# Eight conditioning groups move from the sample attention to the first MLP and the short convolution

## The chip, the cores and the metric

The kernel runs on one core of a Trainium2 chip. The core has a matrix engine (TensorE), a vector engine (VectorE), an activation engine (ScalarE), GpSimd (POOL in the profile) and a sync engine (SP) that issues transfers. All of them run their own instruction streams and meet at semaphores. The metric is the device time of one execution in microseconds.

## The reference

The program is one inference step of a two-layer decoder trunk in fp32. A prompt of 256 tokens and 8 samples of 8 new tokens each (320 tokens in all) pass through the same weights. Model width is 2048, MLP width 8192. Four times (mixer and MLP of layer 0, mixer and MLP of layer 1) the input is normalised and modulated by a vector that depends on the condition `c`:

```python
def ada_modulate(c, w, b):
    m = jax.nn.silu(c) @ w + b                       # (2048) @ (2048 x 6144)
    shift, scale, gate = jnp.split(m[:, None, :], 3, axis=-1)
def modulated_norm(x, g, shift, scale):
    return rmsnorm(x, g) * (1.0 + scale) + shift
for layer in range(2):
    shift, scale, gate = ada_modulate(c, ada_mix_w[layer], ada_mix_b[layer])
    h = modulated_norm(x, norm_mix[layer], shift, scale)
    y = even_mixer(h, ...) if layer == 0 else odd_mixer(h, ...)
    x = x + gate * y
    shift, scale, gate = ada_modulate(c, ada_mlp_w[layer], ada_mlp_b[layer])
    x = x + gate * sq_relu_mlp(modulated_norm(x, norm_mlp[layer], shift, scale), w1, w2)
```

The even mixer is differential attention beside a gated recurrence; for the samples, the attention reads 256 past positions for each sample from a paged cache. The odd mixer is a short convolution: `b, c, x = split(h @ w_in, 3)`, then `(b * conv3(c * x)) @ w_out`. There are nine conditions (one of the prompt, eight of the samples), so each of the four modulations is a product of 9 rows with a 2048 x 6144 matrix: much weight, little arithmetic.

## The kernel before

**Weights of the layers.** Every large product is done with 128x128 stationary tiles in a split form: a weight chunk (128 partitions x 4 x 256 values, 512 KB) lands in one of four `raw` slots (`load`, L346), ScalarE rounds it to `w_hi` (`split`, L537), VectorE writes the rest to `w_lo` (`split`, L885), and TensorE does three products for each tile: hi by hi, hi by lo, lo by hi (`pair`, L1505). A pair is four chunks, 96 matmuls of 320 columns, and gives 256 output columns. Chunks flow on in one order for the whole kernel, counted by the tallies `K`; the sync engine issues them in program order.

**The modulations.** Each of the four is 12 groups of 512 output columns, 48 in all. A group is 16 tiles of 128x512 weights. `ada_tile_in` (L1539) puts tile k in strip k mod 4 of the bank `acc`, with 32 columns of the condition as the stationary part. After 16 tiles ScalarE copies `acc` to `ares` (`ada_out`, L551), TensorE sums the four strips by four small matmuls into `folded` (`fold`, L1565), and VectorE adds the bias and writes `mod` (`ada_bias`, L932). The tiles come by one of two rings. The wide ring has eight slots of two tiles (512 KB each); in this part it lies in the memory of `w_hi` and `w_lo`, so it serves only while no layer weights are split. The narrow ring has four slots of one tile (256 KB) beside the layer weights; its tiles are executed in bursts of four between chunks (`turn_with_ada`, L376, L1095, L1575), one group for 8 chunks.

Where the groups are computed: 8 of the first modulation at the start, 4 more and 4 of the second in the first projection, 8 of the second in the attention (head norms and prompt), 8 of the third in the sample stage, 4 of the third in block 0 of the first MLP and the 12 of the fourth in its blocks 1 to 3. The short convolution and the second MLP compute none.

**The sample stage** (L1765 to L1810 of TensorE, L772 to L779 of ScalarE, L1361 to L1388 of VectorE, L492 to L510 of POOL). For each sample TensorE computes scores against the transposed past keys, VectorE scales and finds the maximum, ScalarE takes the exponential, VectorE normalises, TensorE combines and transposes the two softmaxes, VectorE copies the weights to `s_pt`, and TensorE multiplies them with the value pages. The 16 key transposes of the next sample (`s_keys`) stand between. The next sample's scores wait for the evacuation of this one's weights. POOL issues the pages: value pages of sample b when the values of b - 2 are done, then the key pages of b + 1. Between these steps stand four pieces of a group (`ada(wide_later, ...)`) of four tiles each, and the fold of the group before. The wide slabs are issued by the sync engine when a slot is free; then come the first chunks of the output projection.

**The short convolution** (TensorE L1875 to L1882, ScalarE L843 to L850, VectorE L1449 to L1486): 8 turns of three pairs, 12 chunks each. VectorE forms the product of the first two pairs, runs the three taps, and multiplies with the third pair. Pair 2 uses the bank that also holds `folded`.

Of the kernel before, what the change touches and what calls it, by code (L numbers as in the profile page):

```python
# [13 lines left out]
P = 128  # L14
D = 2048
KT = D // P
# [104 lines left out]
@contextmanager  # L121
def looped(eng, lo, hi, per):

    if hi - lo == 1:
        yield lo
        return
    before = [(t, t.base, t.off) for t in per]
    with eng.Fori(lo, hi) as i:
        for t, base, off in before:
            t.base, t.off = base + i * per[t], off - lo * per[t]  # L130
        yield i
    for t, base, off in before:
        added = t.off - (off - lo * per[t])
        assert added == per[t], f"a turn adds {added}, not {per[t]}"
        t.base, t.off = base, off + (hi - lo) * per[t]

def trunk_kernel(nc, A, O):
    with ExitStack() as ctx:
# [108 lines left out]
        aux = ctx.enter_context(nc.psum_tensor("aux", [P, 2, 512], F32))  # L248
        acc = aux[:, 1, :]
        folded = mm[:, 2, 1, 448:448 + 4 * NC]  # L250

        def C(name, rows=P):
            return const[0:rows, COL[name][0]:COL[name][1]]
# [81 lines left out]
        ADA = [A["ada_mix_w"][0], A["ada_mlp_w"][0], A["ada_mix_w"][1], A["ada_mlp_w"][1]]  # L335
        ADA_B = [ROW["ada_mix_b"], ROW["ada_mlp_b"], ROW["ada_mix_b"] + 48, ROW["ada_mlp_b"] + 48]
        GAIN = [ROW["norm_mix"], ROW["norm_mlp"], ROW["norm_mix"] + KT, ROW["norm_mlp"] + KT]
        MOD_READY = [8, 24, 48, 48]
        H_READY = [0, 8, 12, 16]
        X_READY = [1, 9, 41, 49, 81]  # L340

# [1 line left out]
        def _(sp):  # L343
# [10 lines left out]
            def load_quad(src):  # L354
                for s in range(SLOTS):
                    load(src(s))
# [60 lines left out]
            sp.wait_ge(chunk_used, 80)  # L417
            with looped(sp, 4, GROUPS, {KW: 8}) as g:
                ada_wide(wide_later, 1, g)
            with looped(sp, 0, 8, {KW: 8}) as g:  # L420
                ada_wide(wide_later, 2, g)
            for half in halves:
                for s in (0, 1):
                    load(half(s))
# [25 lines left out]
                    load_quad(slab(W1, 0, after))  # L450

            load_quad(slab(A["mlp_w1"][0], 0, 0))
            feed_with_ada(0, 2, 8, D)
            with looped(sp, 1, BLOCKS - 1, {K: 64, KN: 64}) as b:
                feed_with_ada(b, 3, b * 4 - 4, (b + 1) * D)
            feed_with_ada(3, 3, 8, None)
            with looped(sp, 1, KT // 2 + 1, {K: 12}) as j:
                end = sp.snap(j * COLS)
                for part in (1, 2, 0):
                    load_quad(slab(A["w_in_odd"][0], 0, end + (part * D - COLS)))  # L460
            matrix(A["w_out_odd"][0], 8)
            with looped(sp, 0, BLOCKS, {K: 64}) as b:
                feed_forward(1, b)

# [67 lines left out]
        def _(act):  # L532
# [240 lines left out]
            for b in range(NB):  # L773

                act.wait_ge(s_max, b + 1)
                fn(s_s[:, :], s_s[:, :], ACT.Exp, bias=small[:, 0, 8:9], accum_out=small[:, 0, 9:10]).then_inc(s_exp, 1)
                if b + 1 < NB:
                    s_keys(b + 1)
                ada_out(True)  # L779
            act.wait_ge(s_o, NB)  # L780
            for n in range(4):
                ins = fn(s_kT[:, n // 2, P * (n % 2):P * (n % 2) + P], aux[:, 0, P * n:P * n + P], ACT.Square,
# [26 lines left out]
            squared(0)  # L809
            mixed(3)  # L810
            squared(1)
            act.wait_ge(wide_used, 8 * 24)
            split(1)
            rooted(0)
            split(1)
# [24 lines left out]
            root()  # L840
            norm()
            G.off = 20 + 8 + 32
            with looped(act, 0, KT // 2, {K: 12, G: 3}) as j:  # L843
                split()
                multiplied()
                fn(mtmp[:, 0], mm[:, 0, :, 0:T], ACT.Copy).then_inc(c_copied, 1)
                split(8)
                G.up(3)
                act.wait_ge(pair_free, G.now + 2)
                fn(u_hi[:, bass.ds(j * 2, 2), :], mtmp[:, 1], ACT.Copy).then_inc(u_hi_ready, 1)  # L850
# [20 lines left out]
        def _(dve):  # L871
# [57 lines left out]
            AG, X, R, SQ = Tally(), Tally(), Tally(), Tally()  # L929
            X.off = 1  # L930

            def ada_bias(a, g):  # L932
# [4 lines left out]
                v.tensor_tensor(mod[:, a, bass.ds(g * 4, 4), :], folded.rearrange("p (t c) -> p t c", c=NC), bias,  # L937
                                ALU.add).then_inc(mod_ready, 1)

# [170 lines left out]
            def mlp(n, last, groups=0):  # L1111
                def hidden(r, j):

                    R.up()
                    dve.wait_ge(relu_out, R.now)
                    v.tensor_tensor(mtmp[:, r], mtmp[:, r], mtmp[:, r], ALU.mult).then_inc(u_val, 1)  # L1116
                    U.up()
                    dve.wait_ge(u_hi_ready, U.now)
                    v.tensor_tensor(u_lo[:, bass.ds(j, 2), :], mtmp[:, r], u_hi[:, bass.ds(j, 2), :].bitcast(F32),  # L1119
                                    ALU.subtract).then_inc(u_ready, 1)  # L1120

                def block_(ahead, group=None, squares=False):
                    if group is not None:
                        a, g0 = group
                        with looped(dve, 0, 4, {K: 8, R: 2, U: 2, AG: 1}) as i:
                            turn_with_ada(lambda: hidden(0, i * 4), lambda: hidden(1, i * 4 + 2), a, g0 + i)
                    else:
                        with looped(dve, 0, 4, {K: 8, R: 2, U: 2}) as i:
                            split()
                            hidden(0, i * 4)  # L1130
                            split()
                            hidden(1, i * 4 + 2)
                    if ahead:
                        outward(n, squares)
                    else:
                        with looped(dve, 0, 3, {K: 8, G: 2, X: 2, steps: 2}) as i:
                            split()
                            residual(0, i * 4, n)
                            split()
                            residual(1, i * 4 + 2, n)  # L1140
                        split()
                        residual(0, 12, n)
                        residual(1, 14, n, ahead=0)

                per = {G: 8, R: 8, U: 8, X: 8, steps: 8}
                if groups:
                    block_(1, (2, 8))
                    with looped(dve, 1, BLOCKS - 1, {K: 64, AG: 4, **per}) as b:
                        block_(1, (3, b * 4 - 4))
                    block_(1, (3, 8), squares=True)  # L1150
# [211 lines left out]
            for b in range(NB):  # L1362
# [10 lines left out]
                step(v.tensor_tensor(small[:, 0, 11:12], small[:, 0, 10:11], lam[:, 1:2], ALU.mult))  # L1373
                settle()
                v.tensor_scalar(s_s[:, :], s_s[:, :], small[:, 0, 11:12], None, ALU.mult).then_inc(s_w, 1)
                if b:
                    ada_bias(2, b - 1)
                if b + 1 < NB:
                    s_keys(b + 1)
                dve.wait_ge(s_wT, b + 1)  # L1380
# [1 line left out]
                if b:  # L1382
# [2 lines left out]
                v.tensor_copy(s_pt[:, 0:2, :, now:now + 8], mm[:, 2, 0, 0:P].rearrange("p (a h q) -> p a h q", a=2, h=H))  # L1385
                v.tensor_copy(s_pt[0:TS, 2, :, now:now + 8], mm[0:TS, 2, 0, P:P + 64].rearrange("p (h q) -> p h q", h=H)
                              ).then_inc(s_pte, 1)
            ada_bias(2, NB - 1)  # L1388

            dve.wait_ge(s_root, 1)  # L1390
            step(v.reciprocal(small[:, 1, 12:16], small[:, 1, 12:16]))
# [54 lines left out]
            step(v.memset(c_p[:, :, 0:2], 0.0))  # L1446
            norm()
            Z = Tally()
            with looped(dve, 0, KT // 2, {K: 12, G: 3, U: 1, steps: 5, Z: 1}) as j:  # L1449
                split(8)  # L1450
                multiplied()
                Z.up()
# [23 lines left out]
                            ins = v.scalar_tensor_tensor(out_s, c_s[:, m, :, k:k + DS], w, out_s, ALU.mult, ALU.add)  # L1476
                    step(ins)
                settle()
                split()
                multiplied()  # L1480
                G.up()
                v.tensor_tensor(mtmp[:, 1], mtmp[:, 1], mm[:, 2, :, 0:T], ALU.mult).then_inc(pair_free, 1)
# [15 lines left out]
        def _(pe):  # L1498
# [63 lines left out]
                    ada_tile_in(k, narrow[:, slot, :]).then_inc(narrow_used, 1)  # L1562
                    KN.up()

            def fold():  # L1565

                if not (isinstance(F.now, int) and F.now == 0):
                    pe.wait_ge(mod_ready, F.now)
                F.up()
                pe.wait_ge(ada_copied, F.now)  # L1570
                for t in range(4):
                    ins = mul(folded[:, NC * t:NC * t + NC], ares[:, P * t:P * t + P], C("fold"), True, True)
# [194 lines left out]
            for b in range(NB):  # L1767
# [12 lines left out]
                        h = 2 * j + a  # L1780
                        ins = mul(mm[32 * j:32 * j + 32, 2, 0, PAST:T], s_q[:, h, :], pj[:, 8 + h, SEQ:T], a == 0, a == 1)
                ins.then_inc(s_score, 1)
                if b:
                    fold()
                ada(wide_later, range(2))
                if b + 1 < NB:
                    s_keys(b + 1)
                ada(wide_later, range(2, 4))
                pe.wait_ge(s_w, b + 1)
                for k in range(3):  # L1790

                    rows, at_col = P if k < 2 else TS, 64 * k
                    ins = mul(mm[0:rows, 2, 0, at_col:at_col + 64], s_s[:, P * k:P * k + rows], C("comb"), True, True)
                ins.then_inc(s_wT, 1)
                ada(wide_later, range(4, 6))
                pe.wait_ge(s_pte, b + 1)
                pe.wait_ge(values_in[b % 2], 32 * (b // 2 + 1))
                for half in range(2):
# [7 lines left out]
                                                   keys[:, P * h:P * h + P], start=b == half == k == 0,  # L1806
                                                   stop=b == NB - 1 and k == 2, skip_group_check=True)
                ins.then_inc(s_o, 1)
                ada(wide_later, range(6, 8))
            fold()  # L1810
            pe.wait_ge(mod_ready, F.now)
            pe.wait_ge(s_norm, 1)
            for n in range(4):
# [59 lines left out]
            norm()  # L1873

            def three(inputs=None):  # L1875
                for r in range(3):
                    pair(r, h_hi, h_lo, inputs if r == 0 else None, (pair_free, G.now))

            three(h_inputs(12))
            with looped(pe, 1, KT // 2, {K: 12, G: 3}):  # L1880
                three()
            pair(0, u_hi, u_lo, lambda s: pe.wait_ge(u_ready, 32 + 2 * s + 2))  # L1882

            for j in range(KT):
                bank = aux[0:18, j // 4, :] if j < 8 else mm[0:18, 2, (j - 8) // 4, :]
                ins = turn(bank[:, P * (j % 4):P * (j % 4) + P], stage[:, j, :])
# [51 lines left out]
```

## Time and profile before

| | us |
|---|---|
| median of the runs shown (3301.89 to 3309.1) | 3304.24 |
| the profiled execution, its own time | 3302.08 |
| its span, first to last instruction | 3300.4 |

| engine | busy, us | share |
|---|---|---|
| TensorE matmuls | 3127.5 | 95% |
| VectorE | 1520.6 | 46% |
| ScalarE | 1087.9 | 33% |
| POOL | 29.6 | 1% |

The span is that of one profiled execution. Positions below (as 617 us) count from its start. Busy time of TensorE is modelled for pipelined matmuls. A matmul of plain fp32 operands shows as two instructions, so four conditioning tiles are a row with x8. [...]

### The profile page before, as it was taken

What the parts mean: (1) busy time and instruction counts of PE and PEld (TensorE: products, weight loads), DVE (VectorE), ACT (ScalarE), POOL (GpSimd) and SP (SyncE); (2) the same over time, 40 slices, a digit from 0 to 9 for tenths busy, and PEclk for the clock granted to TensorE, in tenths of its full rate; (3) what the DMA queues carried; (4) which work ended last, traced back from release to release, by engine and by line L of the source; (5) the groups of instructions that cost most, each with busy time, mean ns of one, the idle gap of its engine ahead of it and who ended that gap; (6) DMA issues with size and microseconds to landing.
All of it is one profiled execution on the core that took longest, in us unless ns stands there. A gap on an engine that the chain in (4) does not pass through costs nothing.

```text
span 3300.4 us, 55870 instructions
## 1 busy us (share of the span) xinstructions
PE 3127.5 (95%) x21283; PEld 2857.2 (87%) x21283; DVE 1520.6 (46%) x2047; ACT 1087.9 (33%) x1302; POOL 29.6 (1%) x55
## 2 busy tenths in 40 slices
PE   6899996888899999999999899999899999999998
PEld 2588873448789989989989899999899999999998
DVE  1535656336634434434434554445644444444443
ACT  1324423223433233233233243333433333333332
POOL 0000000000000000000000000000000000000000
PEclk9899997889899999999999999999899999999999
DMA  9777768884475575575575444444344444444443
GB/s 349 245 253 231 231 234 297 305 323 130 146 253 181 177 245 183 177 247 185 173 251 187 133 128 148 151 147 148 114 152 148 147 147 153 147 147 152 143 152 108
DMA packets 512228, 624.34 MB, mean 189 GB/s; under 512 B 22416, under 2 KB 408081, under 8 KB 511444
## 3 DMA queue, kind: packets, MB, share of 16 engines
q1 hardware_dynamic: 504576, 595.68, 55.7%
q0 software_dynamic: 6112, 22.84, 1.9%
q10 hardware_dynamic: 1430, 4.24, 0.4%
q8 instruction: 83, 1.36, 0.2%
q14 instruction: 27, 0.22, 0.0%
HBM read 617.13 MB, written 5.54 MB: 189 GB/s over the span
## 4 chain that ended last, share of the span: by engine, by line
PE 89%; DVE 4%; DMA 4%; ACT 1%; issue 1%; SPq 0%; DVEq 0%; POOL 0%; ACTq 0%; POOLq 0%
PE mm L1503 83%; PE aux L1503 5%; DMA wide_first<-in_ada_mix_w 2%; DMA wide_later<-in_ada_mix_w 2%; DVE a_rr L1279 1%; PE mm L1611 1%; SPq L364 0%; DVE l_g L1407 0%; PE aux L1805 0%; ACT tmp L631 0%; DVE a_qn L1282 0%; DVE pj L1290 0%; DVE p_s L1306 0%; DVE a_t L1288 0%; DVE rstd L944 0%
## 5 line engine op out<-in xcount | busy, mean ns | idle before, releaser
L890 DVE TENSOR_TENSOR w_lo<-raw,w_hi 128x1024 fp32r<-128x1024 f32 x752 | 919.3, 1225 | 1406.2 <-ACT w_hi L544 1404.7
L544 ACT ACTIVATE w_hi<-raw 128x1024 fp32r<-128x1024 f32 x752 | 795.3, 1059 | 1690.3 <-PE mm L1503 1690.3
L1503 PE MATMUL mm<-h_hi,w_hi 128*128 128x320 f32 x3712 | 1166.1, 314 | 47.6 <-DVE h_lo L986 32.3
L1503 PE MATMUL mm<-h_lo,w_hi 128*128 128x320 f32 x3712 | 1152.0, 310 | 0.0
L1503 PE MATMUL mm<-h_hi,w_lo 128*128 128x320 f32 x3712 | 1151.8, 310 | 0.0
L1503 PEld LDWEIGHTS mm<-h_hi,w_hi 128*128 128x128 f32 x3712 | 701.9, 189 | 133.7 <-issue 123.0
L1503 PE MATMUL mm<-u_hi,w_hi 128*128 128x320 f32 x2304 | 712.0, 309 | 0.0
L1503 PE MATMUL mm<-u_lo,w_hi 128*128 128x320 f32 x2304 | 711.9, 309 | 0.0
L1503 PE MATMUL mm<-u_hi,w_lo 128*128 128x320 f32 x2304 | 711.9, 309 | 0.0
L1503 PEld LDWEIGHTS mm<-h_lo,w_hi 128*128 128x128 f32 x3712 | 702.2, 189 | 0.0
L1503 PEld LDWEIGHTS mm<-h_hi,w_lo 128*128 128x128 f32 x3712 | 701.6, 189 | 0.0
L1503 PEld LDWEIGHTS mm<-u_hi,w_hi 128*128 128x128 f32 x2304 | 432.4, 188 | 0.0
L1503 PEld LDWEIGHTS mm<-u_lo,w_hi 128*128 128x128 f32 x2304 | 432.4, 188 | 0.0
L1503 PEld LDWEIGHTS mm<-u_hi,w_lo 128*128 128x128 f32 x2304 | 432.4, 188 | 0.0
L1503 PE MATMUL aux<-wide_later,cs 128*32 128x512 f32 x512 | 95.2, 700 | 15.7 <-DMA wide_later<-in_ada_mix_w 13.7
L1503 PE MATMUL aux<-narrow,cs 128*32 128x512 f32 x768 | 106.6, 609 | 0.0
L1119 DVE TENSOR_TENSOR u_lo<-mtmp,u_hi 128x640 f32 x64 | 52.8, 826 | 67.0 <-ACT u_hi L660 67.0
L1503 PE MATMUL aux<-wide_first,cs 128*32 128x512 f32 x256 | 61.0, 825 | 22.1 <-DMA wide_first<-in_ada_mix_w 21.3
L660 ACT ACTIVATE u_hi<-mtmp 128x640 f32 x64 | 47.3, 739 | 98.6 <-DVE mtmp L1116 98.6
L559 ACT ACTIVATE ares<-aux 128x512 f32<-128x512 f32 x48 | 28.6, 595 | 134.0 <-PE aux L1503 133.8
L1072 DVE SCALAR_TENSOR_TENSOR xT<-mm,mod,xT 128x256 f32 (+1 forms) x160 | 69.4, 475 | 0.0
L1503 PEld LDWEIGHTS aux<-wide_first,cs 128*32 128x32 f32 x256 | 10.5, 133 | 64.9 <-DMA wide_first<-in_ada_mix_w 47.7
(262 smaller groups left out, 1236.5 us busy)
## 6 DMA issues: line engine op xcount, KB each, us to landing
raw<-in_mlp_w SPq DMA_DIRECT2D x512, 512.0 KB, 3.6
narrow<-in_ada_mlp_w SPq DMA_DIRECT2D x256, 256.0 KB, 3.6
raw<-in_w_in_odd SPq DMA_DIRECT2D x96, 512.0 KB, 3.9
raw<-in_w_in_even SPq DMA_DIRECT2D x80, 512.0 KB, 6.6
wide_first<-in_ada_mix_w SPq DMA_DIRECT2D x64, 512.0 KB, 8.8
narrow<-in_ada_mix_w SPq DMA_DIRECT2D x128, 256.0 KB, 4.0
wide_later<-in_ada_mlp_w SPq DMA_DIRECT2D x64, 512.0 KB, 5.1
wide_later<-in_ada_mix_w SPq DMA_DIRECT2D x64, 512.0 KB, 11.2
```

The lines of the kernel that those rows point to most:

```text
L544: fn(w_hi[:, slot], raw[:, slot], ACT.Copy).then_inc(hi_ready, 1)
L559: fn(ares[:, :], acc, ACT.Copy).then_inc(ada_copied, 1)
L660: fn(u_hi[:, bass.ds(j, 2), :], mtmp[:, r], ACT.Copy).then_inc(u_hi_ready, 1)
L890: v.tensor_tensor(w_lo[:, slot], raw[:, slot], w_hi[:, slot].bitcast(F32), ALU.subtract).then_inc(lo_ready, 1)
L1072: ins = v.scalar_tensor_tensor(x, mm[:, r, m, 0:SEQ], g, x, ALU.mult, ALU.add)
L1119: v.tensor_tensor(u_lo[:, bass.ds(j, 2), :], mtmp[:, r], u_hi[:, bass.ds(j, 2), :].bitcast(F32), ALU.subtract).then_inc(u_ready, 1)
L1279: step(v.reciprocal(a_rr[:, i % 2], a_rt[:, i % 2]))
L1503: return nc.tensor.matmul(out, lhsT, rhs, start=first, stop=last)
L1611: return nc.tensor.transpose(out, in_, const[0:rows, 0:rows])
```

## The change

The eight groups of the third modulation leave the sample stage. The first MLP computes the third modulation whole in blocks 0 to 2 and the first four groups of the fourth in block 3; the other eight groups of the fourth are computed in the eight turns of the short convolution, one group a turn, with four tiles before every third chunk and the fold after the eleventh. There the fold writes to another bank (`folded_conv`), since pair 2 uses the old one. The sync engine's order in the convolution becomes four narrow tiles and three chunks, four times a turn.

```diff
+        folded_conv = aux[:, 0, 448:448 + 4 * NC]
-        MOD_READY = [8, 24, 48, 48]
+        MOD_READY = [8, 24, 40, 48]
 # sync
-            with looped(sp, 0, 8, {KW: 8}) as g:
-                ada_wide(wide_later, 2, g)
-            feed_with_ada(0, 2, 8, D)
+            feed_with_ada(0, 2, 0, D)
             with looped(sp, 1, BLOCKS - 1, {K: 64, KN: 64}) as b:
-                feed_with_ada(b, 3, b * 4 - 4, (b + 1) * D)
-            feed_with_ada(3, 3, 8, None)
+                feed_with_ada(b, 2, b * 4, (b + 1) * D)
+            feed_with_ada(3, 3, 0, None)
+            def conv_turn(end, g, after):
+                sources = [slab(W_ODD, 0, end + (part * D - COLS))(s) for part in (2, 0) for s in range(SLOTS)]
+                sources += [after(s) for s in range(SLOTS)]
+                for n in range(4):
+                    ada_narrow(3, g, range(4 * n, 4 * n + 4))
+                    for src in sources[3 * n:3 * n + 3]:
+                        load(src)
...
 # scalar: sample stage, then convolution
-                ada_out(True)
-            act.wait_ge(wide_used, 8 * 24)
+            act.wait_ge(wide_used, 8 * 16)
-                split(8)
+                split(5)
+                ada_out()
+                split(3)
 # vector: sample stage, then convolution
-                if b:
-                    ada_bias(2, b - 1)
-            ada_bias(2, NB - 1)
-                split()
+                split(3)
+                ada_bias(3, j + 4, folded_conv)
+                split(1)
 # tensor: sample stage
-                if b:
-                    fold()
-                ada(wide_later, range(2))
-                ada(wide_later, range(2, 4))
-                ada(wide_later, range(4, 6))
-                ada(wide_later, range(6, 8))
-            fold()
 # tensor: convolution
             def three(inputs=None):
                 for r in range(3):
-                    pair(r, h_hi, h_lo, inputs if r == 0 else None, (pair_free, G.now))
+                    def burst(s):
+                        c = 4 * r + s
+                        if c % 3 == 0:
+                            ada_narrow(range(4 * (c // 3), 4 * (c // 3) + 4))
+                    pair(r, h_hi, h_lo, inputs if r == 0 else None, (pair_free, G.now), before=burst,
+                         between=(lambda s: fold(folded_conv) if s == 2 else None) if r == 2 else None)
...
+            pe.wait_ge(mod_ready, F.now)
             for j in range(KT):     # the 16 transposes of the convolution's new state
```

## Rows read from the trace of the kernel before

**Rows 1.** The page: busy time by engine; the chain of waits by engine.
```profile
PE 3127.5 (95%) x21283; PEld 2857.2 (87%) x21283; DVE 1520.6 (46%) x2047; ACT 1087.9 (33%) x1302; POOL 29.6 (1%) x55
PE 89%; DVE 4%; DMA 4%; ACT 1%; issue 1%; SPq 0%; DVEq 0%; POOL 0%; ACTq 0%; POOLq 0%
```

**Rows 2.** Stretches: length, busy us by engine (PE first), granted clock, DMA share, GB/s.
```profile
555.00:565.00 10.00, 6.98 (x32) 4.30 (x32) 3.77 (x11) 2.73 (x10) 0.00 (x0) 0.50 0.88 310
...
616.00:640.00 24.00, 20.13 (x272) 11.18 (x272) 9.02 (x33) 3.92 (x7) 5.17 (x10) 1.00 0.96 348
...
665.00:680.00 15.00, 11.94 (x128) 6.08 (x127) 2.45 (x11) 1.31 (x4) 2.11 (x4) 0.77 1.04 393
...
1900.95:2244.00 343.05, 343.05 (x2323) 343.05 (x2324) 174.15 (x256) 118.97 (x123) 0.00 (x0) 0.99 0.47 145
...
924.24:958.04 33.80, 33.80 (x234) 29.67 (x233) 13.03 (x13) 11.74 (x14) 0.00 (x0) 1.00 0.77 248
```

**Rows 3.** The chain of waits, 610 to 780 us, shares by line.
```profile
by line: DMA wide_later<-in_ada_mix_w 35.0%; PE mm L1503 19.5%; PE aux L1503 14.3%; DVE l_g L1407 6.0%; PE aux L1805 5.9%; PE mm L1611 5.5%; DVE w_lo L890 3.4%; issue 2.2%; DVE h_lo L1401 1.7%; DVE pj L1409 1.7%; SPq L364 0.9%; ACT h_hi L79
```

**Rows 4.** The chain, in order of time: start, length, what; both MLPs.
```profile
923.25 1.00 PE aux L1503 x8
924.24 7.23 PE mm L1503 x48
...
948.92 8.12 PE mm L1503 x56
...
2379.98 220.59 PE mm L1503 x1504
```

**Rows 5.** Instructions in time, sample 0: start, us, engine, line, operation [idle before].
```profile
617.18 1.07 PE L1503 MATMUL mm<-s_kT,s_q 128*32 128x256 f32 x16 [1.93 <-DVE s_q L1357]
...
618.53 0.42 DVE L1364 TENSOR_SCALAR s_s<-mm 128x256 f32<-128x256 f32 x1 [1.50 <-PE mm L1503]
...
619.76 0.56 ACT L776 ACTIVATE s_s<-s_s,small 128x320 f32<-128x320 f32 x1 [4.33 <-DVE small L1369]
...
620.45 0.16 DVE L1371 RECIPROCAL small<-small 128x1 f32<-128x1 f32 x1 [0.72 <-ACT s_s L776]
...
620.85 0.39 DVE L1375 TENSOR_SCALAR s_s<-s_s,small 128x320 f32<-128x320 f32 x1
...
622.40 0.53 DVE L1357 COPY s_q<-pj 64x32 f32<-64x32 f32 x4
...
623.31 0.21 DVE L1386 COPY s_pt<-mm 64x64 f32<-64x64 f32 x1
...
623.88 0.62 PE L1805 MATMUL aux<-vpage,s_pt 128*32 128x128 f32 x16
...
625.36 0.42 PE L1805 MATMUL aux<-vtok,s_pt 64*32 64x128 f32 x8
```

**Rows 6.** The same view behind the last sample.
```profile
730.80 0.27 ACT L782 ACTIVATE s_kT<-aux 128x128 f32<-128x128 f32 x1
```

**Rows 7.** The same view, sample 3, before and after a pause of TensorE.
```profile
660.34 1.06 PE L1503 MATMUL aux<-wide_later,cs 128*32 128x512 f32 x8
...
667.35 1.92 PE L1503 MATMUL aux<-wide_later,cs 128*32 128x512 f32 x4 [1.86 <-DMA wide_later<-in_ada_mix_w]
...
670.59 1.07 PE L1805 MATMUL aux<-vpage,s_pt 128*32 128x128 f32 x8
...
674.39 0.42 PE L1805 MATMUL aux<-vtok,s_pt 64*32 64x128 f32 x8
```

**Rows 8.** POOL's page issues; landing of the first key pages, then over the kernel.
```profile
626.11 0.53 POOL L508 DMA_DIRECT2D vpage<-in_cache_v  x1 [9.09 <-PE aux L1805]
626.99 0.53 POOL L508 DMA_DIRECT2D vpage<-in_cache_v  x1 [0.36 <-issue]
628.70 1.12 POOL L502 DMA_DIRECT2D kpage<-in_cache_k  x2 [1.18 <-issue]
...
DMA to landing us min/median/max: 3.9/4.2/4.6
...
kpage<-in_cache_k POOLq DMA_DIRECT2D x16, 512.0 KB, 9.0
```

More of the change, by code:

```diff
@@ L452, in _ @@
             load_quad(slab(A["mlp_w1"][0], 0, 0))
-            feed_with_ada(0, 2, 8, D)
+            feed_with_ada(0, 2, 0, D)
             with looped(sp, 1, BLOCKS - 1, {K: 64, KN: 64}) as b:
-                feed_with_ada(b, 3, b * 4 - 4, (b + 1) * D)
-            feed_with_ada(3, 3, 8, None)
-            with looped(sp, 1, KT // 2 + 1, {K: 12}) as j:
+                feed_with_ada(b, 2, b * 4, (b + 1) * D)
+            feed_with_ada(3, 3, 0, None)
+            W_ODD = A["w_in_odd"][0]
+            def conv_turn(end, g, after):
[5 more added lines that the diff above has]
+                        load(src)
+            load_quad(slab(W_ODD, 0, D))
+            with looped(sp, 1, KT // 2, {K: 12, KN: 16}) as j:
                 end = sp.snap(j * COLS)
-                for part in (1, 2, 0):
-                    load_quad(slab(A["w_in_odd"][0], 0, end + (part * D - COLS)))
-            matrix(A["w_out_odd"][0], 8)
+                conv_turn(end, j + 3, slab(W_ODD, 0, end + D))
+            conv_turn(KT // 2 * COLS, 11, slab(A["w_out_odd"][0], 0, 0))
+            matrix(A["w_out_odd"][0], 8, 1)
             with looped(sp, 0, BLOCKS, {K: 64}) as b:
@@ L842, in _ @@
             G.off = 20 + 8 + 32
-            with looped(act, 0, KT // 2, {K: 12, G: 3}) as j:
+            with looped(act, 0, KT // 2, {K: 12, G: 3, AG: 1, AN: 16}) as j:
                 split()
@@ L930, in _, with ada_bias @@
             X.off = 1
-            def ada_bias(a, g):
+            def ada_bias(a, g, out=folded):
                 AG.up()
@@ L936, in ada_bias @@
                 bias = vec[:, bass.ds(g * 4 + ADA_B[a], 4)].unsqueeze(2).broadcast_to([P, 4, NC])
-                v.tensor_tensor(mod[:, a, bass.ds(g * 4, 4), :], folded.rearrange("p (t c) -> p t c", c=NC), bias,
+                v.tensor_tensor(mod[:, a, bass.ds(g * 4, 4), :], out.rearrange("p (t c) -> p t c", c=NC), bias,
                                 ALU.add).then_inc(mod_ready, 1)
@@ L1146, in mlp @@
                 if groups:
-                    block_(1, (2, 8))
+                    block_(1, (2, 0))
                     with looped(dve, 1, BLOCKS - 1, {K: 64, AG: 4, **per}) as b:
-                        block_(1, (3, b * 4 - 4))
-                    block_(1, (3, 8), squares=True)
+                        block_(1, (2, b * 4))
+                    block_(1, (3, 0), squares=True)
                 else:
@@ L1448, in _ @@
             Z = Tally()
-            with looped(dve, 0, KT // 2, {K: 12, G: 3, U: 1, steps: 5, Z: 1}) as j:
+            with looped(dve, 0, KT // 2, {K: 12, G: 3, U: 1, steps: 5, Z: 1, AG: 1}) as j:
                 split(8)
@@ L1563, in ada_narrow, with fold @@
                     KN.up()
-            def fold():
+            def fold(out=folded):
                 if not (isinstance(F.now, int) and F.now == 0):
@@ L1571, in fold @@
                 for t in range(4):
-                    ins = mul(folded[:, NC * t:NC * t + NC], ares[:, P * t:P * t + P], C("fold"), True, True)
+                    ins = mul(out[:, NC * t:NC * t + NC], ares[:, P * t:P * t + P], C("fold"), True, True)
                 ins.then_inc(fold_done, 1)
@@ L1876, in three @@
                 for r in range(3):
-                    pair(r, h_hi, h_lo, inputs if r == 0 else None, (pair_free, G.now))
+                    def burst(s):
[4 more added lines that the diff above has]
+                         between=(lambda s: fold(folded_conv) if s == 2 else None) if r == 2 else None)
             three(h_inputs(12))
-            with looped(pe, 1, KT // 2, {K: 12, G: 3}):
+            with looped(pe, 1, KT // 2, {K: 12, G: 3, F: 1, KN: 16}):
                 three()
             pair(0, u_hi, u_lo, lambda s: pe.wait_ge(u_ready, 32 + 2 * s + 2))
+            pe.wait_ge(mod_ready, F.now)
             for j in range(KT):
```

## The prediction

> **What bounds the kernel now.** I read the page first: its engine totals and the chain of waits. TensorE is busy in 95% of the span and carries 89% of the chain [rows 1], so nearly everywhere a microsecond is won or lost only by changing what TensorE executes. Next I read stretches of the two places that the change touches [rows 2]. The short convolution (from 1900.95 us) is TensorE alone, 343.05 of 343.05 us busy at a granted clock of 0.99, while the transfers take 0.47 of their engines: whatever TensorE gets there is paid in full. The sample stage (617 to 731 us) is the other kind: its transfers stand at 0.96 to 1.04 of the engines, at 348 to 393 GB/s, and TensorE loses 3 to 4 us in each of two stretches of 24 and 15 us. The chain cut to 610 to 780 us says what it waits for: 35.0% of these 170 us, 59.5 us, is the landing of the wide slabs of the conditioning weights [rows 3]. Nothing in this stage reads what those slabs give; it needs only its own cache pages.
>
> So a bandwidth-bound stage gives up work which a TensorE-bound stage takes on. The answer is the difference of two numbers of nearly one size, and each has to be worked out.
>
> **What the convolution pays.** Each of its 8 turns gets 16 narrow tiles in four bursts of 4, a fold of 4 small matmuls, one copy on ScalarE, one bias add on VectorE and 16 DMAs of 256 KB. The first MLP already does just that in turns of 8 chunks, so it has the price. A turn with a group lasts 33.80 us [rows 2]. Plain turns go at 220.59 us for 1504 matmuls, 0.1467 us each [rows 4]; a turn has 8 chunks x 24 = 192, or 28.16 us. The group costs 33.80 - 28.16 = 5.64 us, and eight cost 45.1 us. The lower bound is the pieces of the chain alone: the burst's 1.00 us four times and 8.12 - 7.23 = 0.89 us for the fold [rows 4], 4.9 us a group or 39 us; the upper bound is 6 us a group, 48 us, should a burst or a fold have to wait a little in each turn. I take 5.64, since that row is the very same work.
>
> What hides the rest: ScalarE (118.97 of 343.05 us) and VectorE (174.15) are half idle in the convolution [rows 2], and copy and add sit between splits that are done before TensorE reaches their chunks, with two chunks (7 us) between the last burst and the fold against 0.6 us of copy. On the sync engine's queue a narrow tile waits for the burst before it, and the chunk loads queue behind it; the burst is every third chunk (10.8 us), where the MLP has every second (7.2 us), and there no turn is stretched. Bytes: 12 x 512 KB + 16 x 256 KB in 48 us is 220 GB/s, under the 248 GB/s of the MLP's turn. I cost these at nothing; uncovered, a late chunk would be a few us a turn. The MLP itself keeps 16 groups and is unchanged but for which groups they are. The new wait for the last bias add before the stage transposes has a whole pair (14 us) ahead of it: nothing.
>
> **What the sample stage gives back.** Out go 64 transfers of 512 KB (33.6 MB), 128 tiles, 8 folds, copies and adds. What stays is a serial chain for each sample. Sample 0 ran with pages and slabs already landed [rows 5]: scores from 617.18 us; VectorE from 618.53; ScalarE's exponential from 619.76; VectorE again from 620.45 to 621.24; its key copy and query copies to 622.93; the weights' copies to 623.52; values until 625.36 + 0.42 = 625.78. That is 8.60 us. Without a burst ahead of the combination, the 0.2 us before the weights' copies go, and a later sample adds a 0.22 us memset overlapped to 0.13, so 8.55 us; the next scores follow at once, since their wait is on those copies. Eight give 68.4 us: with every operation at full clock the last values end at 617.18 + 68.4 = 685.6 us. Before, the squares behind the last sample began at 730.80 us [rows 6], after a last burst and copy that also leave. Full gain 45.2 us. This is the convolution's price to within its error: at full clock the change is worth nothing.
>
> Two things can lengthen the 8.55 us. The first is the clock. Stretches with less TensorE work show it: 0.77 in 665 to 680 us, 0.50 in 555 to 565 us [rows 2]. [...] The new sample has TensorE active about 6.2 of 8.55 us: scores 1.3, transposes 1.95, then idle 0.9, combination 0.9, idle 1.4, values 2.1. Bursts filled both pauses before. At half clock, the scores add 1.0 us to the chain, the transposes end 1.15 us past the point where VectorE wants them, and values add 2.1: 4.2 us a sample, 34 us in all. The bounds are therefore 0 and 34 us; I take three tenths, 10.2 us, which is a granted clock of 0.85, between the 1.00 and 0.77 of the nearest rows, as the pauses are shorter than the 1.86 us that preceded the fall. [...]
>
> The second is the pages. Once a sample's values are done, POOL issues two value pages and, 2.6 us later, two key pages (626.11 and 628.70 us) [rows 8]. The key pages are wanted by the transposes of the second next sample's start, about 9.9 us after POOL's release, and at the latest 0.9 us later. Two pages alone landed in 3.9 to 4.6 us; with the slabs around them the median over the kernel is 9.0 us. At the lighter load, the last page is there some 8 us after the release: 2 MB in 8.55 us is 245 GB/s, against 393 reached. About 2 us are to spare, and I cost it at nothing; if landing stayed at 9 us from 629.8, each sample would wait 2 us, 12 us over six samples.
> [...]
>
> **Sum.** Against the profiled execution (span 3300.4 us, own time 3302.08): +45.1 in the convolution, -45.2 at full clock, +10.2 for the clock: +10.1 us, 3312.2 us. The median of the runs shown, 3304.24, lies 2.2 us above that execution; I put the forecast midway, 3313 us. Start and end of the kernel, attention over the prompt and both MLPs stay as they are.
>
> **Rivals.**
> The clock stays full (same): the sample takes 8.55 us; net 45.1 - 45.2 = 0, up to +4 with a spell or two: 3302 to 3306 us. For it: clock 1.00 from 616 to 640 us, with bursts [rows 2]. Against: those bursts go.
> The clock is low for most of the stage: 60% and more, 20 to 34 us, net +20 to +34: 3322 to 3336 us. For it: the 0.50 stretch of the prompt's attention, with longer pauses than here.
> The pages end last: +12 for pages beside some clock loss: about 3316 to 3328 us. Against it: 3.9 to 4.6 us landing when alone.
> Faster: the group costs the convolution only its pieces, 4.9 us, because the bursts' edges overlap the neighbouring matmuls better with three chunks between them. With full clock, that is 39.1 - 45.2 = -6.1 us; a sample chain of 8.3 us gives 2 more, -8: 3294 us. It decides from a group price under about 4.8 us. Against: 33.80 us for the MLP's turn, repeated in turn after turn.
>
> **How the numbers follow.** A measurement of this kernel tells from no change what exceeds 0.2%, 6.6 us. Forecast (part of the stage at half clock, +5 to +16) 0.50; clock full 0.20; clock mostly low 0.10; pages 0.08; faster 0.12. Slower by over 0.2%: 0.38 of the 0.50, all of low clock and 0.07 of pages, 0.55. Faster 0.12, the rest 0.33. The range leaves out the far end of the low clock and most of the faster case: 3298 to 3328 us; the forecast's own is 3307 to 3319.
>
> **What the profile after would show.** Convolution turns of 12 chunks at 42.2 + 5.6 = 47.9 us with TensorE always busy; a stage with no wait for wide slabs and transfers near 245 GB/s; the time from the first scores to the squares 68 us (clock full), about 79 us (forecast) or 100 us (clock low); TensorE's idle ended by VectorE's copies (right) or by page transfers (pages rival). I am wrong if the convolution's turns are under 47 us, if the stage stands at clock 1.00 and 68 us, or if a third place moves by over 3 us.

## The result, and the profile after

| us | before | after |
|---|---|---|
| median of the runs compared | 3303.06 (3298.26 to 3309.1, 4 runs) | 3321.18 (3320.14 to 3323.59, 4 runs) |
| the profiled execution's own time | 3302.08 | 3321.03 |
| its span | 3300.4 | 3319.4 |

The kernel after is slower: ratio 1.0055, 95% interval 1.0037 to 1.0073. The forecast was 3313 us with a range of 3298 to 3328, so sign and range hold, but the step is 18 to 19 us and not 10. Position by position, the two spans compare like this:

| stretch | before, us | after, us | difference |
|---|---|---|---|
| start to the first scores of the samples | 617.18 | 618.67 | +1.5 |
| first scores to the squares (sample stage) | 113.62 | 70.76 | -42.9 |
| squares to the first MLP's first matmul | 157.67 | 158.31 | +0.6 |
| first MLP and the norm behind it | 1012.48 | 1018.06 | +5.6 |
| short convolution, its output, the norm behind it | 472.33 | 515.77 | +43.4 |
| second MLP to the end | 927.12 | 937.83 | +10.7 |
| sum | 3300.4 | 3319.4 | +19.0 |

The two stretches that the change touches cancel to +0.6 us. The two MLPs, which execute the same number of matmuls as before, hold 16.3 of the 19.0 us.

The page after, in the order of [rows 1] (busy time by engine, the chain by engine), with the instruction queue of its third part between them (packets, MB, share):

```profile
PE 3135.1 (94%) x21283; PEld 2859.5 (86%) x21283; DVE 1521.0 (46%) x2047; ACT 1087.9 (33%) x1302; POOL 29.8 (1%) x55
...
q8 instruction: 108, 1.77, 0.2%
...
PE 90%; DVE 5%; DMA 2%; issue 1%; ACT 1%; SPq 0%; DVEq 0%; POOL 0%; ACTq 0%; POOLq 0%
```

The counts of TensorE's matmuls are those of [rows 1], as they should be in a pure move. The landing of the slabs has halved its share of the chain, and yet the whole is longer. One row of the kernel before, which [rows 1] had no use for, belongs beside this: its instruction queue moved 83 packets, and this one 108.

```profile
q8 instruction: 83, 1.36, 0.2%
```

Stretches after, with the columns of [rows 2]: the sample stage, the second turn of the convolution, a full-clock sample and the slow one behind it. The granted clock is TensorE's, as a share of its full speed.

```profile
618.67:689.43 70.76, 53.56 (x800) 36.90 (x800) 29.50 (x106) 11.60 (x24) 11.66 (x22) 0.85 0.51 180
1914.63:1962.51 47.88, 47.88 (x333) 43.75 (x336) 21.06 (x32) 14.64 (x15) 0.00 (x0) 1.00 0.70 220
...
626.73:634.87 8.14, 5.96 (x107) 4.30 (x110) 3.89 (x14) 1.56 (x3) 2.19 (x4) 1.00 0.70 260
634.87:644.26 9.39, 7.21 (x106) 4.77 (x110) 3.89 (x14) 1.56 (x3) 2.10 (x4) 0.84 0.68 226
```

The transfers of the stage fell from 0.96 to 1.04 of the engines [rows 2] to 0.51. The turn is 47.88 us, all of it TensorE.

Inside those two samples, TensorE in time (columns as [rows 5]):

```profile
634.80 1.07 PE L1514 MATMUL mm<-s_kT,s_q 128*32 128x256 f32 x16
...
638.92 0.92 PE L1514 MATMUL mm<-const,s_s 128*128 128x64 f32 x6 [0.93 <-DVE s_s L1387]
641.08 1.00 PE L1811 MATMUL aux<-vpage,s_pt 128*32 128x128 f32 x16 [1.24 <-DVE s_pt L1396]
...
644.19 1.93 PE L1514 MATMUL mm<-s_kT,s_q 128*32 128x256 f32 x16
...
651.54 0.65 PE L1811 MATMUL aux<-vpage,s_pt 128*32 128x128 f32 x16 [1.25 <-DVE s_pt L1396]
...
653.40 1.07 PE L1514 MATMUL mm<-s_kT,s_q 128*32 128x256 f32 x16
```

Both pauses, 0.93 and 1.24 us, end with VectorE's operations (the scaled weights `s_s`, then the copies to `s_pt`); no page ends one, so the pages rival is out. The same 16 value matmuls take 0.65 us at the higher level and 1.00 where the clock falls on the way, and the scores 1.07 or 1.93, as in the pair of [rows 7].

Now the part that I had called unchanged. The chain through the second MLP after (start, length, what):

```profile
2381.57 227.26 PE mm L1514 x1536
2608.83 1.25 issue
2610.08 1.56 PE mm L1514 x9
2611.63 2.27 issue
2613.90 225.76 PE mm L1514 x1527
2839.66 1.58 issue
2841.24 1.55 PE mm L1514 x9
2842.79 2.07 issue
2844.86 225.75 PE mm L1514 x1527
```

And the same piece of the kernel before, where the plain row of [rows 4] comes from:

```profile
2373.28 227.29 PE mm L1503 x1536
2600.57 1.73 issue
2602.29 225.52 PE mm L1503 x1536
2827.81 1.39 issue
2829.20 225.54 PE mm L1503 x1536
```

An MLP is a hardware loop over 4 blocks of 1536 matmuls for TensorE. At each jump back TensorE stops with nothing that it waits for ("issue"). Before, that is one stop of 1.4 to 1.7 us; after, there are two, nine matmuls apart. By the waits view TensorE's "issue" stops from 2300 us to the end add up to:

```profile
PE mm L1514 <- issue: 10.5, 6, 2.3
```

Before, it was 4.6 us in 3. So 5.9 of the 10.7 us are stops. The other 4.8 us is the speed behind them: behind the second stop the matmuls start 0.26 us apart and not 0.15, and the granted clock from 2613.90 to 2616.50 us is 0.54, half speed for nearly all of it,

```profile
2611.18 0.31 PE L1514 MATMUL mm<-h_lo,w_hi 128*128 128x320 f32 x1
2611.32 0.31 PE L1514 MATMUL mm<-h_hi,w_lo 128*128 128x320 f32 x1
2613.90 0.46 PE L1514 MATMUL mm<-h_hi,w_hi 128*128 128x320 f32 x1 [2.27 <-issue]
2614.16 0.47 PE L1514 MATMUL mm<-h_lo,w_hi 128*128 128x320 f32 x1
```

and 9 + 1527 matmuls take 1.56 + 225.76 = 227.32 us, where 1536 took 225.52 before (at the later two jumps the excess is 1.8 and 1.3 us). The first MLP had no stop at its jumps before. After, it has three, each just behind the 824 matmuls that end a block:

```profile
1097.73 2.00 issue
...
1348.15 1.65 issue
...
1598.11 1.31 issue
```

The change adds no TensorE instruction to either loop. What differs is the amount of TensorE code ahead of them, and with it the place where each loop lies in the instruction stream. The instruction queue moves more where there are more stops: 108 packets against 83 (16.4 KB each: 1.36 MB in 83). From these two I took the stops for fetches of instructions; no row names what a stop waits for.

### The profile page after: what moved, and what is told of

Read it like the earlier page. It is cut to its first block, busy times and chain, and to the rows that moved or that the text cites. A ratio compares the mean times of both kernels' runs of the same rounds, so it can differ in the third digit from the quotient of the medians.

```text
span 3319.4 us, 56069 instructions
## 1 busy us (share of the span) xinstructions
PE 3135.1 (94%) x21283; PEld 2859.5 (86%) x21283; DVE 1521.0 (46%) x2047; ACT 1087.9 (33%) x1302; POOL 29.8 (1%) x55
## 4 chain that ended last, share of the span: by engine, by line
PE 90%; DVE 5%; DMA 2%; issue 1%; ACT 1%; SPq 0%; DVEq 0%; POOL 0%; ACTq 0%; POOLq 0%
PE mm L1514 83%; PE aux L1514 6%; DMA wide_first<-in_ada_mix_w 2%; DVE a_rr L1291 1%; PE mm L1622 1%; PE aux L1811 1%; SPq L365 0%; ACT tmp L642 0%; DVE a_qn L1294 0%; DVE pj L1302 0%; DVE s_kT L1364 0%; DVE p_s L1318 0%; DVE l_g L1416 0%; DVE a_t L1300 0%; DVE rstd L956 0%
## 5 line engine op out<-in xcount | busy, mean ns | idle before, releaser
L1514 PE MATMUL aux<-narrow,cs 128*32 128x512 f32 x1024 | 141.6, 610 | 5.0 <-issue 5.0
L1514 PEld LDWEIGHTS aux<-wide_first,cs 128*32 128x32 f32 x256 | 10.2, 134 | 63.6 <-DMA wide_first<-in_ada_mix_w 45.2
L1514 PEld LDWEIGHTS mm<-const,ares 128*128 128x128 f32 x320 | 42.9, 203 | 14.3 <-issue 13.5
L1128 DVE TENSOR_TENSOR mtmp<-mtmp 128x640 f32<-128x640 f32 x64 | 52.4, 819 | 0.0
```

Of the source, the lines that this page charges most:

```text
L1514: return nc.tensor.matmul(out, lhsT, rhs, start=first, stop=last)
```

## Experiments

```diff
+MLP_LOOP = {False: dict(head_slot={mybir.EngineType.PE: 0}), True: dict(head_slot={mybir.EngineType.PE: 0})}
...
-                with looped(pe, 0, BLOCKS, {K: 64, G: 8, R: 8, UB: 8, F: groups, KN: 16 * groups}):
+                with looped(pe, 0, BLOCKS, {K: 64, G: 8, R: 8, UB: 8, F: groups, KN: 16 * groups}, MLP_LOOP[bool(groups)]):
```

> [...] Theory (layout): 16 of the 18 us that the change costs sit in the two MLPs, whose work is the same, as stalls of TensorE's instruction fetch where the block loop jumps back (2.00, 1.65, 1.31 us in the first MLP; 1.25+2.27, 1.58+2.07, 1.83+1.47 us in the second, where the second stall comes after 9 matmuls). With the head at the start of a fetch block the second stall goes: second MLP 937.8 -> 927 us or less, time 3306 to 3311 us. Rival (the moved transfers or the fuller sync queue disturb the MLPs): the same 3321 us, the stalls stay.

Measured: 3298.54 us (3294.85 to 3300.52), ratio to before 0.9982 (0.9973 to 0.9992); the kernel after without this line stood at 1.0055. The chain through the second MLP is one piece:

```profile
2375.31 903.40 PE mm L1517 x6144
```

The page counts 55 instruction packets. The expectation had only the second stop going; all of them went, in the first MLP too (1012.35 us, as in the kernel before), and the time is 7 us below the expected range.

```diff
+MLP_LOOP = {False: dict(hint_back_edge=True), True: dict(hint_back_edge=True)}
```

> [...] Theory (layout): all stalls at the turn of a block go, 5 us in the first MLP and 10 to 12 in the second: 3303 to 3308 us. [...] Rival (transfers): 3321 us.

Measured: 3299.96 us (3294.29 to 3301.47), ratio 0.9983 (0.9973 to 0.9992), and again one piece, of 903.51 us, with 54 instruction packets. Two different options, the same effect, 3 us below the expected range.

**The kernel before, spoiled.** If the place of the loops is the cause, the kernel before must fall to it too, with no group moved.

```diff
+MLP_LOOP = {False: dict(head_slot={mybir.EngineType.PE: 235}), True: dict(head_slot={mybir.EngineType.PE: 235})}
```

> [...] Theory (layout): the kernel before gets the changed kernel's stalls, a double stall in the second MLP (+9 to +11 us) and one or two in the first (+5 to +11 us): 3315 to 3325 us with the sample stage and the convolution untouched. Rival (transfers): 3303 us.

Measured: 3330.33 us (3327.78 to 3331.9), ratio 1.0077 (1.0061 to 1.0094), 111 instruction packets. The chain shows the double stop, in the second MLP

```profile
2390.18 226.80 PE mm L1506 x1536
2616.98 2.08 issue
2619.06 1.56 PE mm L1506 x9
2620.61 1.79 issue
2622.41 226.98 PE mm L1506 x1527
2849.38 1.87 issue
```

and in the first, at each of its three jumps; this is the first of them, with one burst of the narrow ring between the two stops:

```profile
1137.28 2.10 issue
1139.38 1.07 PE aux L1506 x8
1140.44 1.89 issue
```

This is the test that the rival can't pass: 25 us from the place of the code alone. With the heads at slot 235 a second stop stands nine matmuls into the body of the second MLP's loop; the kernel before had none there. The time is 5 us above the expected range: by the profiles the second MLP grew by 11.9 us and the first by 18.8, where I had allowed it 5 to 11.

**The kernel before with the jump announced, and aligned.**

```diff
+MLP_LOOP = {False: dict(hint_back_edge=True), True: dict(hint_back_edge=True)}
```

> The kernel before with the branch hint on both block loops. Theory (layout): the three stalls of the second MLP (1.73, 1.39, 1.45 us) go and the first MLP, which has none, stays: 3298 to 3300 us. If a hint costs more than it saves: 3303 us or more.

Measured: 3297.02 us (3290.97 to 3300.44), ratio 0.9973 (0.9963 to 0.9983), 1 us below the expected range.

And with the line of the first experiment, slot 0, in the kernel before:

> The kernel before, with both block loops of TensorE at the start of a fetch block, as e1 has them; no work is moved. It is the partner of e1_after_slot0: the difference of the two is the move alone. Stage sums from the profiles so far (sample stage 113.6 -> 72.5 us, convolution with its output 472.3 -> 516.3, both MLPs equal) give e1 minus e5 = +1 to +5 us; so e5 at 3294 to 3298 us. Rival (with the stalls gone, the move gains): e5 above e1.

Measured: 3295.76 us (3292.82 to 3300.0), ratio 0.998 (0.997 to 0.9989). So the kernel before also paid for its loops, some 7 us. With that taken out on both sides, the price of the move is what is left between equal options: by medians 3298.54 - 3295.76 = +2.8 us aligned (by spans 3297.1 - 3293.8 = +3.3) and 3299.96 - 3297.02 = +2.9 us announced. The announced pair is from one set; the aligned pair is not, and each against the kernel before of its own set leaves +0.8 us. All of it is within 0.2%, no change that can be told.

**The stage without its groups, and nothing in their place.** The aligned kernel before, minus the eight groups of the third modulation; they are computed nowhere, and their columns of `mod` are zero.

```diff
-            with looped(sp, 0, 8, {KW: 8}) as g:
-                ada_wide(wide_later, 2, g)
...
-                if b:
-                    fold()
-                ada(wide_later, range(2))
...
-                ada(wide_later, range(2, 4))
...
-                ada(wide_later, range(4, 6))
...
-                ada(wide_later, range(6, 8))
-            fold()
```

> As e5, but the eight groups of the sample stage are left out and computed nowhere (their columns of the third modulation are zeros): the removal alone. Theory: the stage from the first scores to the squares falls from 113.6 to 68 to 74 us (8.14 us a sample at full clock, 65 us, and some spells at half clock), nothing else moves: 40 to 45 us under e5, 3250 to 3257 us. Rival: part of the gain is given back later, in the output projection or by the first MLP's loads: under 38 us.

Measured: 3254.72 us (3250.03 to 3257.44), ratio 0.9852 (0.9836 to 0.9869). This splits the +2.8 us in its two terms: leaving the stage gives 3295.76 - 3254.72 = 41.0 us, entering the convolution costs 3298.54 - 3254.72 = 43.8 us (medians of two sets; by the profiles the stretch of the convolution grew from 472.58 to 516.27 us, 43.7). The stage itself fell from 113.40 to 73.67 us. The stage's clock is low here as well, so the low clock comes with the emptier stage and not with anything in the convolution:

```profile
615.25:688.92 73.67, 55.95 (x800) 37.26 (x800) 29.49 (x106) 11.60 (x23) 11.58 (x22) 0.82 0.48 172
```

**The pauses filled.** The aligned kernel after, with four small matmuls of constants into the unused `acc` in each of the two pauses of a sample (8 in the rows, two for each, as the 24 groups of 16 tiles from the narrow ring are 768 rows in the kernel before). They add work to TensorE and nothing else.

```diff
+            def filler():
+                for k in range(4):
+                    ada_strip = slice(32 * k, 32 * k + 32)
+                    mul(acc[ada_strip, :], cs[:, k, :], const[:, 0:GCOLS], True, True)
```

> As e1, with two bursts of four meaningless matmuls (cs by const into the idle bank acc, 1.0 us each) for each sample, one ahead of the combination and one ahead of the values, where TensorE pauses; no transfers. Theory (clock): TensorE's pauses let its clock fall in some samples; filled, the clock stays at 1.00 and the stage lasts 65 to 67 us instead of 72.5: 5 to 7 us under e1. Rival (the long samples of the stage are late pages): no change, or longer by the bursts.

Measured: 3291.5 us (3287.03 to 3296.39), ratio 0.9966 (0.9956 to 0.9976), 7.0 us under the same kernel without them by medians of two sets, and some 5 us when each is held against the kernel before of its own set. The stretch of its stage:

```profile
615.55:680.16 64.61, 60.99 (x928) 35.28 (x928) 29.49 (x106) 11.61 (x24) 11.72 (x22) 1.00 0.56 197
```

TensorE is busy 61.0 us and not 53.6, the clock is 1.00 throughout, and the stage is 6.2 us shorter than the 70.76 us of the kernel after (and 7.9 than the 72.48 us of the aligned one). The clock's price is shown by itself, and best by the stage. It also shows what the move is worth at full clock: 3291.5 - 3295.76 = -4.3 us against the aligned kernel before (one set; 0.13%, at the edge of what the intervals can tell).

**Work that counts in the pauses.** If small matmuls in the pauses keep the clock, useful ones may do so too: two of the eight groups, four tiles a sample in the second pause, can stay there as the filler, with a quarter of the slabs' bytes. The convolution then has six turns with a group and two without.

```diff
             # sync
+            with looped(sp, 0, 2, {KW: 8}) as g:
+                ada_wide(wide_later, 2, g)
             # tensor, sample stage
+                if b == 4:
+                    fold()
...
                 pe.wait_ge(s_w, b + 1)
...
+                ada(wide_later, range(2 * (b % 4), 2 * (b % 4) + 2))
                 pe.wait_ge(s_pte, b + 1)
...
             # tensor, convolution
-            with looped(pe, 1, KT // 2, {K: 12, G: 3, F: 1, KN: 16}):
+            with looped(pe, 1, 6, {K: 12, G: 3, F: 1, KN: 16}):
                 three()
+            with looped(pe, 6, 8, {K: 12, G: 3}):
+                three(with_group=False)
```

> As e1, but two groups of the third modulation stay in the sample stage (one burst of four tiles a sample, in the pause ahead of the values, from wide slabs) and six groups of the fourth run in the convolution's first six turns. Pages and slabs are 25.2 MB, 64 us at 393 GB/s, so the stage should hold 66 to 76 us and the convolution gives back 2 x 5.6 = 11.3 us: 8 to 14 us under e1, 3285 to 3291 us, under both given kernels. Rival: the slabs delay the pages and the stage grows by 11 us or more: no gain on e1.

Measured: 3283.86 us (3283.66 to 3285.34), ratio 0.9941 (0.9924 to 0.9958): 0.6% under the kernel before. Part of that is the aligned loops; against the aligned kernel before, from the same set, it is 3295.76 - 3283.86 = 11.9 us, 0.4%. The time is 1 us below the expected range. The convolution gives back 516.27 - 504.78 = 11.5 us, two groups at 5.7, and the stage takes 68.16 us:

```profile
617.16:685.32 68.16, 56.04 (x874) 35.57 (x874) 29.82 (x107) 13.14 (x26) 11.71 (x22) 0.97 0.68 248
```

That is 3.0 us over 8 samples at 8.14. I put those down to the clock at 0.97 first, and tried it.

**The first pause filled too.** As above, with a burst of constants (448 columns, into a free part of `mm`) ahead of the combination of each sample but the fifth.

```diff
+                if b != 4:
+                    filler()
                 pe.wait_ge(s_w, b + 1)
```

> As e8, with one burst of four meaningless matmuls ahead of the combination of every sample but the fifth. In e8 the stage lasts 68.2 us at a granted clock of 0.97, where e7 with two bursts a sample has 64.6 us at 0.99. Theory (clock): what is left over 65 us in e8 is half-clock time, so e9 takes 2 to 3.5 us off: stage 65 to 66 us, 3280 to 3282 us. Rival (late key pages behind the wide slabs): the stage stays at 68 us, 3283 to 3285 us.

Measured: 3284.59 us (3281.09 to 3286.96), ratio 0.9935 (0.9919 to 0.9951); the stage takes 67.78 us at a clock of 0.97 again. The stage gained 0.4 us where 2 to 3.5 were expected, and the time, which can't be told from that of the kernel without this filler, stayed in the rival's range. What the traces hold is late pages, for the larger part of the 3.0 us. The waits in the stage of the kernel that keeps two groups (engine, what, waited for: us, times, longest):

```profile
PEld mm L1652 <- DMA kpage<-in_cache_k: 3.9, 3, 2.6
...
PE mm L1652 <- DMA kpage<-in_cache_k: 3.4, 3, 2.4
```

and in time, the longest of them:

```profile
658.88 0.41 PE L1544 MATMUL mm<-pj,s_q 128*32 128x64 f32 x16
661.68 1.97 PE L1652 MATMUL mm<-const,kpage 128*128 128x128 f32 x16 [2.39 <-DMA kpage<-in_cache_k]
```

The sample with this wait takes 9.85 us and not 8.14. The two shorter waits cost 0.1 us together, and so does the fold in the fifth sample. With filler in the first pause the waits are 2.8 us in three. That the pages of these samples queue behind the slabs that stay is argued from the waits; no run here changes only the order of slabs and pages.

The other 1.2 us is the clock after all, in the last sample. It has no key transposes of a next sample, so TensorE pauses for 2.83 us ahead of its combination, and the clock falls:

```profile
675.99:685.32 9.33, 6.50 (x100) 3.45 (x96) 2.33 (x9) 1.25 (x4) 0.00 (x0) 0.82 0.01 2
```

With filler that pause is still 2.07 us, the clock of the last sample 0.82 and its length 9.38 us, so this filler did not reach the part that the clock still cost. With two bursts of 512 columns in each sample (the pauses filled, above) the last pause was 1.97 us and the last sample ran at full speed.

## Why the prediction was right or wrong

**The convolution's price: right in the mechanism, some 1.5 us high.** A turn with a group is 47.88 us as forecast, a turn without 42.24, so the group costs the 5.64 us of the MLP's turn. But eight groups cost 43.4 to 43.8 us and not 45.1. The first burst of the first turn needs no layer input, and it runs while the norm still holds TensorE, which accounts for 1.0 us of the difference, the time of a burst at full clock:

```profile
1856.24 1.94 PE L1514 MATMUL aux<-narrow,cs 128*32 128x512 f32 x8
1865.80 0.60 PE L1514 MATMUL mm<-h_hi,w_hi 128*128 128x320 f32 x1 [7.62 <-DVE h_lo L998]
```

The costs at nothing (copies, add, sync queue, bytes, the new wait) held: the turn has no idle time, at 220 GB/s.

**The sample's own chain: 8.14 us, not 8.55.** From the scores to the values' start it took 641.08 - 634.80 = 6.28 us and the values 653.40 - 651.54 = 1.86 us at full clock. The sum was read from sample 0 [rows 5], where a burst of eight conditioning rows stands between the weights' copies and the values (copies end at 623.52, values start at 623.88). That burst leaves with the groups, and I had taken out the time ahead of the copies but not this one. Eight samples make 65.1 us, so the full-clock gain is 48.5 us and not 45.2; the stage with filled pauses, 64.61 us at a clock of 1.00, bears it out.

**The clock: direction right, term 5.6 us and not 10.2.** 70.76 - 65.1 = 5.6 us. The granted clock of 0.85 came out just as forecast, but it is worth less time than I gave it: I took three tenths of 4.2 us a sample. Four samples lose nothing at all. Three are at the lower level for a part, either in the values or in the scores and transposes, and lose about 1 us each (9.39, 9.21 and 9.08 us against 8.14). Only the last runs all its matmuls at the lower level, and it takes 689.43 - 678.75 = 10.68 us, 2.5 more. It has no transposes, so the forecast for it is 3.1 and not 4.2. Piece by piece, the scores cost the chain the 1.07 us that I gave them (7.35 us to the values' start and not 6.28). The values cost 689.43 - 686.10 = 3.33 us and not 1.86, 1.5 more where I had 2.1. The transposes cost nothing where I had 1.15: in the one slow sample shown they take 2.71 us and not 1.97, less than double since the clock rises again on the way, and still end 0.19 us before VectorE releases the combination.

The 5.6 us is one execution's. The same stage took 72.48 us in the profile of the aligned kernel after, 73.61 with the jump announced and 73.67 without the groups, with other samples at the lower level, so the term lies between 5.6 and 8.5 us.

The prediction sets the pauses beside one of 1.86 us, which stands in [rows 7], with a granted clock of 0.64 from 666 to 670 us, and takes three tenths because they are shorter. Here pauses of 0.93 and 1.24 us went with a fall as well, and activity put back into them took 7.9 us off the stage.

**The pages: right.** No sample of the kernel after waits for one. The 2 us to spare were not much, though: with a quarter of the slabs back, three samples wait. Nor do POOL's own pauses hold them up. Between the value pages it has one of 0.36 us by "issue" in the whole stage, before as after. Ahead of the key pages in [rows 8] stand 1.18 us, also by "issue". In the kernel after, 1.17 or 1.18 us stand there ahead of every pair of key pages issued in the stage, put down to "issue" or to TensorE's transposes, and the pages come in time all the same.

**"Start and end of the kernel, attention over the prompt and both MLPs stay as they are": the step that failed.** Both MLPs became longer, by 5.6 and 10.7 us. The last line of the prediction had this case (a third place that moves by over 3 us) as a sign of being wrong, without a price. The row was there to be read: [rows 4] ends at 2379.98 with 1504 matmuls at full speed, and the chain of the kernel before goes on with "issue" of 1.4 to 1.7 us at each jump back. I read the shares, where "issue" is 1% [rows 1], and did not ask what these stops hang on. The place of the loop in the instruction stream sets them, as slots 0 and 235 show. I take it that code ahead of a loop moves that place; with this change the stops became double in the second MLP, and single ones came to the first.

Put together with the measured terms and nothing else: +43.4 - 42.9 + 16.3 + 2.1 (start, and the part between the squares and the MLP) = +18.9 us. Without the loops' 16.3 it would have been some +2.7, as the kernels with equal options have it, and the rival "the clock stays full" (3302 to 3306 us) would have named the time though not the reason: the clock did fall. So the forecast of +10 us came near by luck: its two terms in the stage were off by -3.3 and -4.6 us and that of the convolution by -1.7, and what was measured beyond +2.7 us comes from a cost that it did not have. The stated range of 3298 to 3328 us would hold either time.

Still open: what a place between the two does, and why the kernel before had one stop at each jump of one MLP and none in the other. Slots 0 and 235 are the only ones set on purpose; no run shows where the given kernels' own loops stand.

## What to carry to other kernels

When a change adds or removes instructions ahead of a long hardware loop, read the chain at the loop's jumps: the stops by "issue" there came and went in this kernel with the loop's place alone (3295.76 us at slot 0, 3330.33 us at slot 235), and a change that adds nothing to the loops took them from 3 to 9. Align or announce such loops on both sides before comparing two kernels, or the code's place (here up to some 35 us) drowns the effect that is being measured. When an engine's filler work leaves a latency-bound stage, price the stage by its serial chain at both clock levels, and consider leaving just enough useful work to fill the pauses.

## What the runs showed of the hardware

- One kernel, the same instructions: 3295.76 us with its two block loops at slot 0 and 3330.33 us at slot 235. The stop at a jump back takes 1.25 to 2.10 us, a second one behind it 0.96 to 2.27. In the kernel before one came at each jump of the second MLP, after the change two; and behind a second stop in the second MLP TensorE runs for a while at half speed, another 1.3 to 1.8 us each (1.8 to 3.0 with slot 235).
- Instruction packets tell it on the page: 54 to 58 in all kernels without stops, 83 in the kernel before, 108 and 111 with double stops.
- Pauses of 0.93 and 1.24 us in a sample of 8.14 us went with a granted clock of the stage of 0.82 to 0.85. With 16 more matmul rows a sample it stayed at 1.00, and the stage with more work took 7.9 us less time.
